# A two-layer block on one core: the delta rule's triangular systems are solved with beta on their diagonal, and the sixteen products with beta, their loads and the scaled copies go

## The chip, the cores and the metric

The kernel runs on one NeuronCore of a Trainium2 chip, in one launch. The metric is device time in microseconds (us); before the change three runs gave 2293.9, 2294.9 and 2297.77, median 2294.9. One more execution was recorded by the hardware profiler, and everything about single instructions comes from that one.

## What is computed

Input x is 1024 tokens by 1024 channels, float32. Two layers follow each other. The first has a mixer (windowed attention with 8 heads beside a gated delta rule with 4 heads of 128 channels, run forward and backward) and a feed-forward of 4096 units; the second has a pooling, a convolution and a stick-breaking attention branch. The change lies in the first layer's mixer, apart from two waits in the second layer. The delta rule, for each direction and head, in chunks:

```
gc    = cumsum(g)                        # log decay, per token
decay = exp(gc[t] - gc[s])   for s <= t
A     = beta[t] * (k k^T)[t,s] * decay   for s < t
T     = (I + A)^-1                       # lower triangular
w     = T (beta * k * exp(gc)),   u = T (beta * v)
v_new = u - w S;   o = (q exp(gc)) S + (q k^T * decay) v_new
S     = S exp(gc[last]) + (k exp(gc[last]-gc))^T v_new
```

The attention's softmax has a sink logit for each head: m = max(row maximum, sink), weights exp(x - m), and exp(sink - m) joins the sum.

## The kernel before, in words

**Engines and order.** Every piece of work is a step with a name and a key, such as `a1` with (direction d, unit i). `second_layer`, `first_layer` and `build` list the steps with an engine, a rank, and where needed a ring of PSUM banks (`ring`, `frees`) and an order on the same engine (`behind`). `Plan.settle` (L258) then plays all steps through with costs out of `Rehearsal` (L130) and a fixed lag per engine (`LAG`, L199): of the steps that can start it takes the earliest, then the lowest rank. What comes out is one fixed order for each of the five engine queues (TensorE, ScalarE `act`, VectorE `dve`, GpSimd `pool`, SyncE `sp`, which issues all DMAs). On the chip each queue runs strictly in that order and waits on semaphores; a step that waits holds up all that stand behind it on its engine. `SHIFT` (L41) adds small numbers to the ranks of certain steps.

**Stages.** P1 are the projections of layer 1, large products in three float32r passes each (L639, L641, L643). They end 306 us into the span. While they run, the decays are computed and the 32 by 32 diagonal blocks of all triangular systems are solved on VectorE (`lmul`, `zi`, `sol`, `zt`), 128 partitions by 32 by 32 for each direction, one column after the other; the inverses go to DRAM and come back (`inv_out`, `inv_in`). From 306 to about 533 us no large product runs: the delta rule's eight units of 128 tokens in two directions and the attention's eight blocks have TensorE for themselves. From 533 us on follow P3 (output projection), the feed-forward, and the second layer, with large products nearly throughout.

**A unit (d, i).** Sixteen of them, two deep in buffers for each direction (`M.unit`, L250):
- loads: `gcl` brings -gc as a row for each head, spread over 128 partitions, into EB; `bel` brings beta in the same way into AT; `kkl` brings k k^T from `kk_scr` into the one tile `kkL`, and waits until the `a1` of the unit before has read that tile (L2386).
- VectorE: `dd` (L1495) forms D from EB and the mask; `a1` (L1500) multiplies AT by kkL; `a2` (L1538) multiplies AT by D; `qkm` (L1545, L1550) does the same for q k^T. ScalarE: `ebx` (L1156, L1158) takes the exponentials of EB and of D, one instruction for each of the four heads.
- `tex` on GpSimd (L2119) spreads the 32-blocks of the inverse into T and its transpose TT. Levels 32 and 64 then join blocks: TensorE `la` (L761 or L768), VectorE `lp`, TensorE `lb`, VectorE `lt` (L1573, L1577), TensorE `lx` (a transpose, L748), ScalarE `ltt` (L1161) back into TT. At the last level `ltt` copies in four instructions, each scaled with one head's beta (L1168); `copy` is L1005 in the profile.
- the chain over units: `cR`, `cr` (L1585), `cT`, `cn`, `crk`, `co`, `cO` (L1596, L1599), `ckd`, `cs` (L1607, L1610). The heads' products all stand under L716, except `co` (L814, L815). The last four units of each direction end with a norm: `gsq` (L1195), `gs` (L825), `gr` (L1009, L1011), `gn` (L1617).

**Attention.** For a block n: `aqk` (L836), `am` (L1629: adds the bias, takes the maximum), `as1` (L1636, L1638, L1639: maximum with the sink, its negative, sink minus maximum), `ae` (L1207), `as2`, `ap` on GpSimd (L2145), `atr` (L844), `atc`, `apv` (L854).

The first steps of `Plan` that matter for both are the lags:

```
LAG = {"pe": 250.0, "act": 200.0, "dve": 150.0, "pool": 150.0, "sp": 1900.0}
```

Of the kernel before, what the change touches and what calls it, by code (L numbers as in the profile page):

```python
# [106 lines left out]
def v4(ps):  # L107
    return ps[:, :].rearrange("p (j c) -> p j c", j=4)
# [238 lines left out]
class Memory:  # L347


    def __init__(self, nc, A, ctx):  # L350
# [9 lines left out]
        def scratch(name, shape):  # L360
            return nc.dram_tensor(name, shape, F32, kind="Internal").ap()
# [34 lines left out]
        self.qk_scr, self.kkL = scratch("qk_scr", [8, 128, 512]), at(220.5, [128, 4, 128])  # L396
# [602 lines left out]
def scalar_engine(e, q, K):  # L999
# [152 lines left out]
    def ebx(d, i):  # L1152
        n = i if d == 0 else 7 - i
        EB, D = M.unit(d, i, "EB"), M.unit(d, i, "D")
        q.wait_ge(done("dd", d, i), done("gd"))
        e.activation(EB[:, :, :], EB[:, :, :], ACT.Exp, scale=-1.0).then_inc(*tick("ebx", d, i))  # L1156
        for j in range(4):
            a = e.activation(D[:, j, :], D[:, j, :], ACT.Exp, bias=G["ngc"][:, n, 4 * d + j:4 * d + j + 1])  # L1158
        a.then_inc(*tick("ebx", d, i))

    def ltt(d, i, l):  # L1161
        n, TT, ps = i if d == 0 else 7 - i, M.unit(d, i, "TT"), K.prep_bank("lx", d, i, l)
        q.wait_ge(done("lx", d, i, l))
# [236 lines left out]
def vector_engine(e, q, K):  # L1400
# [96 lines left out]
    def a1(d, i):  # L1497
        AT = M.unit(d, i, "AT")[:, :, :]
        q.wait_ge(done("kkl", d, i), done("bel", d, i))
        tt(AT, AT, M.kkL[:, :, :], ALU.mult).then_inc(*tick("a1", d, i))  # L1500

    def lmul(d):

        L = M.L[:, d]
        beta = M.gS[:, d, 0, :]
        q.wait_ge(done("lex", d), done("gS", d))
        tt(L, L, beta.unsqueeze(1 if d else 2).broadcast_to([128, 32, 32]), ALU.mult).then_inc(*tick("lmul", d))
        q.wait_ge(part("lmul", (d,), 1), *[done("kk_in", n) for n in range(8)])
        tt(L, L, M.kkS[:, :, :], ALU.mult).then_inc(*tick("lmul", d))

    def zi():

        q.wait_ge(done("cv", 11), *[done("kk_out", n) for n in range(5, 8)])
        e.memset(M.Z[:, :, :, :], 0.0).then_inc(*tick("zi"))
        q.wait_ge(part("zi", (), 1))
        for d in range(2):
            last = e.memset(M.Z[:, d].rearrange("p a b -> p (a b)")[:, 0:1024:33], 1.0)
        last.then_inc(*tick("zi"))
# [448 lines left out]
    def ss(a, i, p_):  # L1967
# [121 lines left out]
    return dict(pads=pads, idle=idle, nacc=nacc, x1l=x1l, cv=cv, kn=kn, ga=ga, gc=gc, gd=gd, lmul=lmul, zi=zi, sol=sol, zt=zt, dd=dd, a1=a1, a2=a2, qkm=qkm, lp=lp, lt=lt, cr=cr, cO=cO, cs=cs,  # L2089
# [114 lines left out]
def sync_engine(e, q, K):  # L2204
# [296 lines left out]
    return dict(wp=wp, wpre=wpre, wpair=wpair, wb=wb, xl=xl, hst=hst, ho=ho, hx2=hx2, c0=c0, c1=c1, x=x, rows=rows, hb=hb, oh=oh, wload=wload, b3=b3, gT_out=gT_out, qa_out=qa_out, z_out=z_out, kk_out=kk_out, kk_in=kk_in, gS=gS, inv_out=inv_out, inv_in=inv_in, gcl=gcl, bel=bel, kkl=kkl, qk_out=qk_out, qk_in=qk_in, abias=abias,  # L2501
# [7 lines left out]
class Kernel:  # L2509
# [347 lines left out]
def signals(B, K):  # L2857
# [19 lines left out]
    g["bel"] = lambda d, i: f"d_be{d}{i % 2}"  # L2877
    g["kkl"] = "d_xl0"
# [16 lines left out]
PARTS = dict(mp=0, fsq=2, wc=2, nr=2, kr=2, gb=5, ebx=2, gr=2, fr=2, qx=2, na=2, nc=2, gq=2, se=2, cv=4, gc=5, gd=2, lmul=2, sol=2, lex=2, zi=2, ge=2, kk_in=4, gS=2, inv_out=4, inv_in=2, as1=2, as2=2, cz=3, pf=2, ss=3)  # L2895
# [3 lines left out]
def first_layer(p, K):  # L2899
# [70 lines left out]
    for i in range(8):  # L2970
        for d in range(2):
# [4 lines left out]
            add("sp", "bel", d, i, rank=r + PREP_RANK.get((d, i), 0))  # L2976
# [158 lines left out]
def second_layer(p, K):  # L3135
# [33 lines left out]
    for i in range(4):  # L3169
# [3 lines left out]
        for p_, (qb, k0, k1) in enumerate(PIECES):  # L3173
# [9 lines left out]
            add("pe", "sv", i, p_, rank=3)  # L3183
# [226 lines left out]
```

## Time and profile before

| | value |
|---|---|
| median of 3 runs | 2294.9 us (2293.9 to 2297.77) |
| profiled execution, first to last instruction (span) | 2291.9 us |
| TensorE matmul busy | 2247.2 us, 98% |
| TensorE weight loads busy | 1785.5 us, 78% |
| VectorE busy | 1594.7 us, 70% |
| ScalarE busy | 1112.9 us, 49% |
| GpSimd busy | 1030.9 us, 45% |
| DMA | 289.43 MB, mean 126 GB/s |

The profile gives no time of its own for the profiled execution beyond its span; the median of the runs is 3.0 us above that. Times in the trace are microseconds from the start of the span. A busy share is that of an engine's instructions, waits of its queue left out. PEclk is the TensorE clock that was granted, as a share of full speed. SPq is the queue that issues DMAs. Square brackets at the end of a row of the timeline give the idle time in front of it and who ended it.

### The profile page before, as it was taken

How to read it: one execution, taken by the hardware profiler on the slowest of the kernel's cores; microseconds unless marked ns; L12 is line 12 of the kernel's file. 1: busy time of each engine (PE TensorE's matmuls, PEld its weight loads, DVE VectorE, ACT ScalarE, POOL GpSimd, SP SyncE). 2: the span in 40 equal slices, each digit the busy share in tenths (PEclk: the TensorE clock that was granted, in tenths of full speed). 3: DMA queues.
4: the chain of work that ended last, by engine and by line, in shares of the span. 5: the costliest groups of instructions: out<-in, count | busy, mean ns of one | idle time of the engine just before them, and what ended most of it. 6: DMA issues, size and time to landing. Idle time of an engine off the chain costs nothing.

```text
span 2291.9 us, 31262 instructions
## 1 busy us (share of the span) xinstructions
PE 2247.2 (98%) x11389; PEld 1785.5 (78%) x11389; DVE 1594.7 (70%) x2217; ACT 1112.9 (49%) x2008; POOL 1030.9 (45%) x643
## 2 busy tenths in 40 slices
PE   9999989999999999999999999999999999999999
PEld 6778867677878888887887777777777888888886
DVE  7865768776596554689449798888888655545745
ACT  5554157674364555444446365645433322225553
POOL 2212245444247666657767211111123765556663
PEclk9999999999999999999999999999999999999999
DMA  4113353344325443955452301111123343338554
GB/s 160 40 44 99 122 177 107 98 139 158 109 93 188 161 152 133 314 173 166 143 170 83 124 29 46 47 46 47 56 79 124 134 143 111 111 133 294 183 171 147
DMA packets 153764, 289.43 MB, mean 126 GB/s; under 512 B 34915, under 2 KB 44387, under 8 KB 153612
## 3 DMA queue, kind: packets, MB, share of 16 engines
q1 hardware_dynamic: 153612, 287.44, 38.3%
q8 instruction: 91, 1.49, 0.3%
q14 instruction: 61, 0.50, 0.1%
HBM read 207.88 MB, written 79.51 MB: 125 GB/s over the span
## 4 chain that ended last, share of the span: by engine, by line
PE 84%; DVE 8%; ACT 2%; issue 2%; DMA 2%; POOL 1%; SPq 0%; DVEq 0%; POOLq 0%; ACTq 0%
PE bank L869 12%; PE bank L871 12%; PE bank L867 12%; PE bank L639 12%; PE bank L643 11%; PE bank L641 11%; PE bank L716 2%; PE bank L932 2%; PE bank L963 1%; PE bank L945 1%; ACT t L1005 1%; DVE t L1434 1%; DVE t L1974 1%; PE bank L836 1%; PE bank L854 1%
## 5 line engine op out<-in xcount | busy, mean ns | idle before, releaser
L2100 POOL TENSOR_TENSOR t<-t,t 128x512 fp32r<-128x512 f32 (+1 forms) x494 | 810.5, 1652 | 1068.3 <-ACT t L1005 1062.1
L1005 ACT ACTIVATE t<-t 128x512 fp32r<-128x512 f32 (+1 forms) x689 | 448.3, 676 | 653.5 <-PE bank L871 276.3
L639 PE MATMUL bank<-t,t 128*128 128x512 f32 x1360 | 548.5, 403 | 0.0
L643 PE MATMUL bank<-t,t 128*128 128x512 f32 x1360 | 531.4, 391 | 1.1 <-DVE t L1434 0.6
L641 PE MATMUL bank<-t,t 128*128 128x512 f32 x1360 | 530.1, 390 | 1.7 <-POOL t L2100 1.7
L867 PE MATMUL bank<-t,t 128*128 128x512 f32 x1316 | 514.2, 391 | 6.2 <-DVE t L1818 4.6
L869 PE MATMUL bank<-t,t 128*128 128x512 f32 x1316 | 513.3, 390 | 1.4 <-POOL t L2100 1.4
L871 PE MATMUL bank<-t,t 128*128 128x512 f32 x1316 | 513.1, 390 | 0.7 <-DVE t L1434 0.7
L639 PEld LDWEIGHTS bank<-t,t 128*128 128x128 f32 x1360 | 255.7, 188 | 62.7 <-issue 12.7
L643 PEld LDWEIGHTS bank<-t,t 128*128 128x128 f32 x1360 | 255.3, 188 | 58.3 <-POOL t L2100 1.3
L641 PEld LDWEIGHTS bank<-t,t 128*128 128x128 f32 x1360 | 255.9, 188 | 56.3 <-issue 4.6
L867 PEld LDWEIGHTS bank<-t,t 128*128 128x128 f32 x1316 | 247.7, 188 | 59.6 <-DVE t L1818 5.0
L869 PEld LDWEIGHTS bank<-t,t 128*128 128x128 f32 x1316 | 247.6, 188 | 54.2 <-POOL t L2100 3.0
L871 PEld LDWEIGHTS bank<-t,t 128*128 128x128 f32 x1316 | 247.6, 188 | 52.4 <-DVE t L1434 1.1
L1434 DVE TENSOR_TENSOR t<-t,t 128x512 fp32r<-128x512 f32 x192 | 193.4, 1025 | 76.0 <-ACT t L1005 75.3
L1005 ACT ACTIVATE t<-bank 128x512 f32<-128x512 f32 (+2 forms) x255 | 143.1, 578 | 200.0 <-PE bank L945 51.4
L2050 DVE TENSOR_TENSOR t<-t,bank 128x512 f32<-128x512 f32 x105 | 70.3, 682 | 108.3 <-PE bank L871 107.9
L1974 DVE TENSOR_TENSOR_SCAN t<-t,t 128x512 f32<-128x512 f32 (+3 forms) x96 | 112.5, 1171 | 3.3
L1425 DVE TENSOR_TENSOR t<-t,t 128x512 f32<-128x512 f32 x55 | 70.2, 1277 | 25.9 <-ACT t L1382 14.8
L1452 DVE SCALAR_TENSOR_TENSOR t<-t,t,t 128x1024 f32<-128x1024 f32 x48 | 76.3, 1593 | 14.1 <-ACT t L1005 12.8
L1734 DVE TENSOR_TENSOR t<-t,bank 128x512 f32<-128x512 f32 x48 | 32.8, 685 | 61.6 <-PE bank L643 54.5
L716 PEld LDWEIGHTS bank<-t,t 128*128 128x128 f32 x416 | 51.8, 197 | 16.8 <-ACT t L1005 4.6
(250 smaller groups left out, 2641.2 us busy)
## 6 DMA issues: line engine op xcount, KB each, us to landing
t<-in_w SPq DMA_DIRECT2D x87, 512.0 KB, 3.6
hid_scr<-t SPq DMA_DIRECT2D x112, 256.0 KB, 2.1
t<-hid_scr SPq DMA_DIRECT2D x112, 256.0 KB, 2.7
t<-in_wf SPq DMA_DIRECT2D x80, 256.0 KB, 3.3
t<-in_wf SPq DMA_DIRECT2D x36, 512.0 KB, 4.5
g_scr<-t SPq DMA_DIRECT2D x36, 512.0 KB, 2.9
t<-g_scr SPq DMA_DIRECT2D x72, 256.0 KB, 3.4
t<-in_wo SPq DMA_DIRECT2D x24, 512.0 KB, 3.6
```

The lines of the kernel that those rows point to most:

```text
L639: e.matmul(ps[:, :], hi[:, w, :], XH[:, x, hs], start=k == 0, stop=False)
L641: e.matmul(ps[:, :], lo[:, w, :], XH[:, x, hs], start=False, stop=False)
L643: last = e.matmul(ps[:, :], hi[:, w, :], XL[:, x, hs], start=False, stop=k == j.nk - 1)
L716: last = e.matmul(ps[:, 128 * j:128 * j + 128], a(j), b(j), start=True, stop=True)
L867: e.matmul(ps, hi, XH, start=start, stop=False)
L869: e.matmul(ps, lo, XH, start=False, stop=False)
L871: return e.matmul(ps, hi, XL, start=False, stop=stop)
L1005: return e.activation(out, in_, ACT.Copy, **kw)
L1434: return tt(out, x, high.bitcast(F32), ALU.subtract)
L1452: stt(y[:, :] if j < 4 else dst, raw[:, j:j + S], w, y[:, :], ALU.mult, ALU.add).then_inc(*tick("cv", m))
L1974: e.tensor_tensor_scan(x[:, ::-1], one_c.broadcast_to([128, nk]), m_[:, ::-1], 0.0, ALU.mult, ALU.add).then_inc(*tick("ss", a, i, p_))
L2100: return e.tensor_tensor(out, x, high.bitcast(F32), ALU.subtract)
```

## The change

- `lmul` multiplies L by beta along its rows for both directions (direction 1 had it along the columns), and `zi` puts beta, out of `gS`, on the diagonal of the start matrix Z instead of 1. The solved blocks are then (I + A)^-1 diag(beta), in a form in which AT needs no beta, and neither does the last copy into TT.
- `bel` and `a1` are gone, sixteen of each. `kkl` loads k k^T straight into AT, with the waits that `bel` had, and in its place in the list; the tile kkL is gone, and `kkl` has semaphores of its own by direction and parity. `a2` waits for `kkl`.
- The last `ltt` is one copy of 128 by 512 instead of four scaled ones of 128 by 128, sixteen times.
- `as1` has two instructions instead of three: the negative sink is made once in `gc` (a sixth instruction there), and min(-max, -sink) gives the negated maximum at once.
- In the second layer `ss` waits for all `st` of the piece two before, not for the last alone, and `sv` is bound to come behind the `sv` of the piece before.
- All ranks and shifts are as they were.

```diff
     def ltt(d, i, l):
-        n, TT, ps = i if d == 0 else 7 - i, M.unit(d, i, "TT"), K.prep_bank("lx", d, i, l)
         q.wait_ge(done("lx", d, i, l))
-        if l < TOP:
-            a = copy(TT[:, :, :], v4(ps))
-        else:
-            for j in range(4):
-                a = copy(TT[:, j, :], ps[:, 128 * j:128 * j + 128], scale=G["beta"][:, n, 4 * d + j:4 * d + j + 1])
-        a.then_inc(*tick("ltt", d, i, l))
+        copy(M.unit(d, i, "TT")[:, :, :], v4(K.prep_bank("lx", d, i, l))).then_inc(*tick("ltt", d, i, l))
...
         e.reciprocal(G["beta"], w[:, :, :]).then_inc(*tick("gc"))
+        ts(M.rows[:, 32:40], M.rows[:, 16:24], -1.0, None, ALU.mult).then_inc(*tick("gc"))
...
-    def a1(d, i):
-        AT = M.unit(d, i, "AT")[:, :, :]
-        q.wait_ge(done("kkl", d, i), done("bel", d, i))
-        tt(AT, AT, M.kkL[:, :, :], ALU.mult).then_inc(*tick("a1", d, i))
...
-        tt(L, L, beta.unsqueeze(1 if d else 2).broadcast_to([128, 32, 32]), ALU.mult).then_inc(*tick("lmul", d))
+        tt(L, L, beta.unsqueeze(2).broadcast_to([128, 32, 32]), ALU.mult).then_inc(*tick("lmul", d))
...
-        q.wait_ge(part("zi", (), 1))
+        q.wait_ge(part("zi", (), 1), done("gS", 0), done("gS", 1))
         for d in range(2):
-            last = e.memset(M.Z[:, d].rearrange("p a b -> p (a b)")[:, 0:1024:33], 1.0)
+            last = e.tensor_copy(M.Z[:, d].rearrange("p a b -> p (a b)")[:, 0:1024:33], M.gS[:, d, 0, :])
...
-        q.wait_ge(done("ebx", d, i), done("a1", d, i))
+        q.wait_ge(done("ebx", d, i), done("kkl", d, i))
         tt(AT, AT, D, ALU.mult).then_inc(*tick("a2", d, i))
...
-        q.wait_ge(done("rows"))
-        tt(sm[:, :, 8:12], sm[:, :, 0:4], sink, ALU.max).then_inc(*tick("as1", n))
+        q.wait_ge(done("rows"), done("gc"))
+        stt(sm[:, :, 12:16], sm[:, :, 0:4], -1.0, below, ALU.mult, ALU.min).then_inc(*tick("as1", n))
         q.wait_ge(part("as1", (n,), 1))
-        ts(sm[:, :, 12:16], sm[:, :, 8:12], -1.0, None, ALU.mult)
-        tt(sm[:, :, 16:20], sink, sm[:, :, 8:12], ALU.subtract).then_inc(*tick("as1", n))
+        tt(sm[:, :, 16:20], sink, sm[:, :, 12:16], ALU.add).then_inc(*tick("as1", n))
...
-            q.wait_ge(done("st", i0, PIECES[p0][0], (PIECES[p0][2] - 1) // 256))
+            q.wait_ge(*[done("st", i0, PIECES[p0][0], g) for g in range(PIECES[p0][1] // 256, (PIECES[p0][2] + 255) // 256)])
...
-    def bel(d, i):
+    def kkl(d, i):
         n = i if d == 0 else 7 - i
-        q.wait_ge(done("gT_out"))
+        q.wait_ge(done("kk_out", n))
         if i >= 2:
             q.wait_ge(done("la", d, i - 2, TOP))
         if i in (1, 2):
             q.wait_ge(*[done(*y) for y in K.p1_x])
         elif i == 0:
             q.wait_ge(*([done("inv_out")] if d else []), done("whi", 21), done("wlo", 21))
-        start(flat(M.unit(d, i, "AT")[:, :, :]), M.row_of(8 * n + 4 * d), "bel", d, i)
-
-    def kkl(d, i):
-        n = i if d == 0 else 7 - i
-        q.wait_ge(done("kk_out", n))
-        if (d, i) != (0, 0):
-            q.wait_ge(done("a1", *((0, i) if d else (1, i - 1))))
-        start(flat(M.kkL[:, :, :]), M.kk_scr[n], "kkl", d, i)
+        start(flat(M.unit(d, i, "AT")[:, :, :]), M.kk_scr[n], "kkl", d, i)
...
-            add("sp", "bel", d, i, rank=r + PREP_RANK.get((d, i), 0))
+            add("sp", "kkl", d, i, rank=r + PREP_RANK.get((d, i), 0))
...
-            add("dve", "a1", d, i, rank=r + PREP_RANK.get((d, i), 0))
-            add("sp", "kkl", d, i, rank=r + PREP_RANK.get((d, i), 0))
...
-            add("pe", "sv", i, p_, rank=3)
+            add("pe", "sv", i, p_, rank=3, behind=[("sv", K.piece_before(12 * i + p_, 1))] if i or p_ else ())
```

## Rows read from the trace of the kernel before

**Rows 1.** The page, busy time of each engine

```profile
PE 2247.2 (98%) x11389; PEld 1785.5 (78%) x11389; DVE 1594.7 (70%) x2217; ACT 1112.9 (49%) x2008; POOL 1030.9 (45%) x643
```

**Rows 2.** Windows by stage: us, busy of each engine (count), PEclk, DMA share, GB/s

```profile
0.00:300.00 300.00, 295.68 (x1398) 234.79 (x1399) 208.38 (x245) 142.80 (x190) 67.43 (x33) 1.00 0.30 96
300.00:545.00 245.00, 223.14 (x1911) 166.84 (x1910) 181.30 (x453) 164.52 (x459) 117.32 (x69) 0.97 0.45 138
545.00:2292.00 1747.00, 1728.34 (x8084) 1383.83 (x8082) 1204.98 (x1520) 805.57 (x1361) 846.13 (x542) 1.00 0.39 130
```

**Rows 3.** TensorE's waits, 300 to 545 us: total, times, longest

```profile
PE bank L768 <- DVE t L1538: 5.2, 1, 5.2
PE bank L716 <- DVE t L1607: 2.9, 1, 2.9
PE bank L836 <- DVE t L1629: 2.5, 3, 1.2
PE bank L825 <- ACT t L1195: 2.5, 1, 2.5
```

**Rows 4.** Timeline, 307 to 320 us, the stretch of the longest wait

```profile
307.32 2.84 SPq L2209 DMA_DIRECT2D t<-gT_scr  x5
312.08 2.76 SPq L2209 DMA_DIRECT2D t<-kk_scr  x1
...
315.45 0.69 DVE L1495 SCALAR_TENSOR_TENSOR t<-t,t 128x512 f32<-128x512 f32 x1 [2.01 <-DMA t<-gT_scr]
316.18 0.63 ACT L1156 ACTIVATE t<-t 128x512 f32<-128x512 f32 x1 [0.90 <-DVE t L1495]
...
318.09 0.60 ACT L1005 ACTIVATE t<-bank 128x512 f32<-128x512 f32 x1
318.83 1.09 PE L768 MATMUL bank<-t,t 64*64 64x64 f32 x8 [5.19 <-DVE t L1538]
319.85 3.76 PE L716 MATMUL bank<-t,t 128*128 128x128 f32 x16
```

**Rows 5.** Timeline, TensorE at full clock

```profile
434.66 2.05 PE L716 MATMUL bank<-t,t 128*128 128x128 f32 x16
```

**Rows 6.** VectorE groups, 255 to 545 us: busy us, mean ns, idle before

```profile
L1500 DVE TENSOR_TENSOR t<-t,t 128x512 f32<-128x512 f32 x16 | 15.6, 975 | 6.4 <-DMA t<-kk_scr 3.3 <-DMA t<-gT_scr 2.9
```

**Rows 7.** VectorE groups, 300 to 545 us

```profile
L1638 DVE TENSOR_SCALAR t<-t 128x8 f32<-128x8 f32 x8 | 3.5, 434 | 0.3
```

**Rows 8.** Timeline, ScalarE: a scaled copy in four instructions

```profile
327.19 1.13 ACT L1005 ACTIVATE t<-bank,t 128x128 f32<-128x128 f32 x4
```

**Rows 9.** Timeline, VectorE and TensorE around the second longest wait

```profile
449.17 1.18 DVE L1638 TENSOR_SCALAR t<-t 128x8 f32<-128x8 f32 x1
...
452.10 1.16 PE L716 MATMUL bank<-t,t 128*128 128x128 f32 x8 [2.90 <-DVE t L1607]
```

**Rows 10.** Timeline, GpSimd and VectorE together

```profile
337.95 3.74 POOL L2145 TENSOR_TENSOR t<-t,t 128x1024 f32<-128x1024 f32 x2 [2.83 <-DVE t L1646]
339.88 2.36 DVE L1500 TENSOR_TENSOR t<-t,t 128x512 f32<-128x512 f32 x1
```

**Rows 11.** Timeline, the two products after kkL loads, direction 1 unit 1

```profile
323.20 0.68 DVE L1500 TENSOR_TENSOR t<-t,t 128x512 f32<-128x512 f32 x1
326.32 0.69 DVE L1538 TENSOR_TENSOR t<-t,t 128x512 f32<-128x512 f32 x1
```

**Rows 12.** Timeline: start matrix Z, load of gS, last copy of unit (0,0)

```profile
198.15 1.76 DVE L1514 MEMSET t<- 128x2048 f32 x1 [5.65 <-DMA kk_scr<-t]
199.08 2.57 SPq L2209 DMA_DIRECT2D t<-gT_scr  x4
...
298.36 1.14 ACT L1005 ACTIVATE t<-bank,t 128x128 f32<-128x128 f32 x4 [3.23 <-PE bank L748]
```

**Rows 13.** Windows of 10 us, same columns as rows 2

```profile
320.00:330.00 10.00, 10.00 (x78) 8.91 (x80) 6.92 (x21) 4.34 (x12) 5.20 (x4) 0.83 0.67 203
450.00:460.00 10.00, 7.90 (x78) 6.36 (x80) 9.04 (x24) 7.67 (x24) 5.43 (x5) 0.83 0.23 78
```

More of the change, by code:

```diff
@@ L395, in __init__ @@
         self.gT_scr, self.bias_scr = scratch("gT_scr", [128, 128]), scratch("bias_scr", [8, 512])
-        self.qk_scr, self.kkL = scratch("qk_scr", [8, 128, 512]), at(220.5, [128, 4, 128])
+        self.qk_scr = scratch("qk_scr", [8, 128, 512])
         self.U = []
@@ L1152, in ebx @@
     def ebx(d, i):
+        EB, D = M.unit(d, i, "EB"), M.unit(d, i, "D")
         n = i if d == 0 else 7 - i
-        EB, D = M.unit(d, i, "EB"), M.unit(d, i, "D")
         q.wait_ge(done("dd", d, i), done("gd"))
@@ L1632, in as1 @@
     def as1(n):
-        sm, sink = M.sm[n % 2], M.rows[:, 16:24].rearrange("p (g j) -> p g j", g=2)
+        sm, (sink, below) = M.sm[n % 2], [M.rows[:, a:a + 8].rearrange("p (g j) -> p g j", g=2) for a in (16, 32)]
         q.wait_ge(*[done("am", g, n, j) for g in range(2) for j in range(4)])
-        q.wait_ge(done("rows"))
-        tt(sm[:, :, 8:12], sm[:, :, 0:4], sink, ALU.max).then_inc(*tick("as1", n))
+        q.wait_ge(done("rows"), done("gc"))
+        stt(sm[:, :, 12:16], sm[:, :, 0:4], -1.0, below, ALU.mult, ALU.min).then_inc(*tick("as1", n))
         q.wait_ge(part("as1", (n,), 1))
-        ts(sm[:, :, 12:16], sm[:, :, 8:12], -1.0, None, ALU.mult)
-        tt(sm[:, :, 16:20], sink, sm[:, :, 8:12], ALU.subtract).then_inc(*tick("as1", n))
+        tt(sm[:, :, 16:20], sink, sm[:, :, 12:16], ALU.add).then_inc(*tick("as1", n))
     def as2(n):
@@ L2087, in ofd @@
         tt(M.xr[:, m, :], M.xr[:, m, :], M.OF[:, m, :], ALU.add).then_inc(*tick("ofd", h, m))
-    return dict(pads=pads, idle=idle, nacc=nacc, x1l=x1l, cv=cv, kn=kn, ga=ga, gc=gc, gd=gd, lmul=lmul, zi=zi, sol=sol, zt=zt, dd=dd, a1=a1, a2=a2, qkm=qkm, lp=lp, lt=lt, cr=cr, cO=cO, cs=cs,
+    return dict(pads=pads, idle=idle, nacc=nacc, x1l=x1l, cv=cv, kn=kn, ga=ga, gc=gc, gd=gd, lmul=lmul, zi=zi, sol=sol, zt=zt, dd=dd, a2=a2, qkm=qkm, lp=lp, lt=lt, cr=cr, cO=cO, cs=cs,
                 gn=gn, am=am, as1=as1, as2=as2, ao=ao, yal=yal, zm=zm, gg=gg, evd=evd, hac=hac, hac2=hac2, x2l=x2l, xn=xn, tx=tx, tl=tl, ws=ws, fu2=fu2, fu3=fu3, fc11=fc11, fu4=fu4, fc22=fc22, fc21=fc21, fc12=fc12, ft3=ft3, ft2=ft2,
@@ L2096, in gpsimd_engine @@
     M, B, p = K.mem, K.bulk, K.plan
-    done, part, tick = p.done, p.part, p.tick
+    C, done, part, tick = M.C, p.done, p.part, p.tick
     def low(out, x, high):
@@ L2113, in tex @@
     def tex(d, i):
-        c, own = M.C32[2 * d + i % 2], M.C("own32").rearrange("p (k b) -> p k b", b=32).unsqueeze(1).broadcast_to([128, 4, 4, 32])
+        c, own = M.C32[2 * d + i % 2], C("own32").rearrange("p (k b) -> p k b", b=32).unsqueeze(1).broadcast_to([128, 4, 4, 32])
         def spread(name, f):
@@ L2499, in o1 @@
         start(K.out[:, m, 512:1024], M.xr[:, m, :], "o1", m)
-    return dict(wp=wp, wpre=wpre, wpair=wpair, wb=wb, xl=xl, hst=hst, ho=ho, hx2=hx2, c0=c0, c1=c1, x=x, rows=rows, hb=hb, oh=oh, wload=wload, b3=b3, gT_out=gT_out, qa_out=qa_out, z_out=z_out, kk_out=kk_out, kk_in=kk_in, gS=gS, inv_out=inv_out, inv_in=inv_in, gcl=gcl, bel=bel, kkl=kkl, qk_out=qk_out, qk_in=qk_in, abias=abias,
+    return dict(wp=wp, wpre=wpre, wpair=wpair, wb=wb, xl=xl, hst=hst, ho=ho, hx2=hx2, c0=c0, c1=c1, x=x, rows=rows, hb=hb, oh=oh, wload=wload, b3=b3, gT_out=gT_out, qa_out=qa_out, z_out=z_out, kk_out=kk_out, kk_in=kk_in, gS=gS, inv_out=inv_out, inv_in=inv_in, gcl=gcl, kkl=kkl, qk_out=qk_out, qk_in=qk_in, abias=abias,
                 aq=aq, aout=aout, ya=ya, zl=zl, hx=hx, xs=xs, plw=plw, ys1=ys1, g_out=g_out, p_out=p_out, s_out=s_out, by=by, bg=bg, gld=gld, xr=xr,
@@ L2876, in signals @@
     g["gcl"] = lambda d, i: f"d_gc{d}{i % 2}"
-    g["bel"] = lambda d, i: f"d_be{d}{i % 2}"
-    g["kkl"] = "d_xl0"
+    g["kkl"] = lambda d, i: f"d_kk{d}{i % 2}"
     g["qk_out"] = lambda d, i: f"d_wb{i}" if d == 0 else f"d_blk{4 + i}"
@@ L2892, in signals @@
     return g
-PARTS = dict(mp=0, fsq=2, wc=2, nr=2, kr=2, gb=5, ebx=2, gr=2, fr=2, qx=2, na=2, nc=2, gq=2, se=2, cv=4, gc=5, gd=2, lmul=2, sol=2, lex=2, zi=2, ge=2, kk_in=4, gS=2, inv_out=4, inv_in=2, as1=2, as2=2, cz=3, pf=2, ss=3)
+PARTS = dict(mp=0, fsq=2, wc=2, nr=2, kr=2, gb=5, ebx=2, gr=2, fr=2, qx=2, na=2, nc=2, gq=2, se=2, cv=4, gc=6, gd=2, lmul=2, sol=2, lex=2, zi=2, ge=2, kk_in=4, gS=2, inv_out=4, inv_in=2, as1=2, as2=2, cz=3, pf=2, ss=3)
 PARTS["or"] = 2
```

2 rows, old and new, of the table SIGNALS are left out of this document.

## The prediction

> **What bounds the kernel.** I read the page first: TensorE's matmuls are busy 2247.2 of 2291.9 us [rows 1]. Nothing in the change takes a matmul away, so all that it can give or take lies in the 44.7 us in which TensorE is not busy, and in the time that it runs at a lower clock. Windows by stage show where these are [rows 2]: 0 to 300 us has 4.3 us of idle TensorE, 300 to 545 us has 21.9, the remaining 1747 us have 18.7. Everything that the change edits in the units and in the attention runs in the middle stage. There the large products are absent, VectorE is busy 181.3 of 245 us and ScalarE 164.5, and only there is the mean granted clock under 1 (0.97).
>
> TensorE's waits in that stage come next [rows 3]. One wait is 5.2 us, one 2.9, one 2.5 (the last norm, L825). The last is L836 behind `am` (L1629), 2.5 us in three waits. The ten smaller groups of the view have 8.4 us, which makes 21.5, the idle time of the stage but for 0.4. In those ten VectorE has 0.7 us, ScalarE 5.2 in eight waits of at most 1.0, the rest are loads and TensorE itself. So without the 5.2 and the last norm's 2.5, waits behind VectorE are 6.1 us (2.9 + 2.5 + 0.7), behind ScalarE 5.2.
>
> The 5.2 us wait is named after `a2` (L1538), but the timeline shows a second thing that ended with it [rows 4]: a ScalarE copy out of a bank, 318.09 to 318.69, 0.14 us ahead of the matmul. By the order in the code that is `qkc`, which frees the bank that `lb` needs. It stands behind `ebx` on ScalarE, that waits for `dd` (L1495), and `dd` for a load of gT_scr that came at 315.4 us; it is one of the burst of five issued between 307.3 and 310.2, behind the last large product. Behind the wait sixteen L716 matmuls took 3.76 us, where sixteen at full clock took 2.05 [rows 4, 5]; the window 320 to 330 stands at 0.83 [rows 13].
>
> **Part by part.**
>
> `a1` goes: sixteen instructions, 15.6 us of VectorE busy [rows 6], fourteen of them in the stage. The third instruction of `as1` goes: eight of L1638, 3.5 us [rows 7]. Of the two that stay one changes from two operands to three at 128 by 8; I take no difference (bounds: 0.1 us either way for each, eight times, from the two small forms around it). `gc` gets one more instruction of 8 columns at 189 us, where VectorE waits for others: nothing; if uncovered, 0.2 us once. VectorE so loses about 19 us of work, a tenth of what it does in the stage.
>
> How much of the 15.6 is work? An `a1` took 0.68 us alone [rows 11] and 2.36 beside a GpSimd product of 3.74 us [rows 10]. Sixteen at 0.68 are 10.9, so 4.7 us are time in which the instruction stood. That time may pass to the instruction that comes next: I count 11 to 15.6 us and use it only as a share, so the sum hardly moves. The Trainium skill, in SBUF — State Buffer, "SBUF: two separate sides", says that the port pair which VectorE and GpSimd share is an exclusive lock, held for a whole instruction, and that a VectorE instruction with two SBUF inputs blocks against a GpSimd one that reads SBUF. By that rule the 4.7 us are not saved where `a2` or `qkm`, with two SBUF inputs too, takes the place of `a1` beside the same GpSimd product; VectorE's gain would be 11 us and not 15.6.
>
> `ltt` at the last level: four scaled copies take 1.13 us together, one whole copy 0.60 [rows 4, 8]. Sixteen times 0.53 is 8.5 us of ScalarE, a twentieth of its work in the stage, and 0.53 us on the way from `lx` to `cT` of each unit.
>
> Loads: sixteen `bel` of 256 KB go, with their issues on SyncE. `kkl` is now where `bel` was and waits for no `a1`. At the burst this changes little in front: still one `gcl` and one 256 KB load into AT for each unit ahead of the `gcl` on which `dd` waits. So I leave the 5.2 us wait and its slow clock where they are, value 0; bounds 0 and -6.9 (5.2 + 3.76 - 2.05). What does move is unit (1,1): its k k^T load is issued at 312.08, after the bias loads, since kkL was not free [rows 4]; its `a1` ran at 323.2 and its `a2` at 326.3 [rows 11]. In the place of `bel` it is issued near 308 and should be there with the others near 315 to 316, so `a2` of that unit can come some 8 us earlier. TensorE is busy 10.0 of 10 us from 320 to 330 [rows 13], so this is spare time first, and pays only where TensorE waits later.
>
> `zi` now waits for gS, which is issued from 199.1 to 201.7 [rows 12]. The plan will put the step later, and its memset of 1.76 us may then lie ahead of the first `lmul` instead of in an idle stretch. The solve ends at most 1.8 us later. What hides that: unit (0,0) had its last copy done at 299.5 [rows 12], and its chain starts only behind the last large product near 306. So it costs 0, and at most 1.8 if that cover were gone. `lmul` has the same shape: nothing. The waits added in `ss` are on steps that TensorE does in this order anyway, and `sv` was already in the order of pieces: nothing, bound 0.5 us each way.
>
> **The sum.** The 2.9 us wait ended with `cs` (L1607), and L1638, 1.18 us long, stands in VectorE's unbroken run ahead of it [rows 9]: 1.2 us less. The window there is at clock 0.83 [rows 13]; with a shorter wait between none and the 1.7 us (3.76 - 2.05) that the clock cost behind the longest wait comes back: I take 0.4, near the lower end, since the wait gets shorter and does not go. The remaining 3.2 us behind VectorE and 5.2 behind ScalarE (8.4) shrink with the load. Bounds: 0 if each is set by TensorE's own result, 8.4 if all go. A tenth and a twentieth less work let me take a sixth: 1.4. Together 1.2 + 0.4 + 1.4 = 3.0 us. The span goes from 2291.9 to 2288.9; the median of the runs lies 3.0 us above the span, so 2291.9 us.
>
> **Rivals.**
> (B) *The freed load pays in full.* The plan is made anew, `a2` of (1,1) and all that hangs on it come 8 us earlier, `qkc` slips in front of `ebx`. For it: ScalarE stood idle from 315.28 to 316.18 for that `dd` [rows 4]; if the bank was full by then, a copy put there ends at 315.9 and not at 318.7, 2.8 us earlier. Of the 8.4 us of waits below, 4 could go instead of 1.4, which is 2.6 more. Against: ranks are the same, and `ebx` had the better claim before. 3.0 + 2.8 + 2.6 is 8.4 us: 2286.5.
> (C) *A new in-order wait.* One queue gets a step whose load lands later than the plan holds. The plan counts 1.9 us and the bytes from issue to landing, the load behind the longest wait took between 5 and 8 (issued in the burst from 307.3 to 310.2, there at 315.4). Without `a1`, nothing separates the arrival of k k^T from `a2`, and VectorE's queue is re-sorted, so `a2` or a `dd` can come to stand ahead of an `am`, a `cr` or a `cs` on which a bank depends. It decides where the load lands over 2 us after its place in the queue is reached. One such wait is priced by the one in the trace: 5.2 us and 1.7 of slow clock, 6.9 us. Time 2301.8. For it: the stage has three such waits already, so the order is near this edge. Against: VectorE and the DMA queues have less to do.
> (D) *Nothing.* TensorE is 91% busy in the stage, and most waits follow TensorE's own results within a unit; the units run two deep, so the freed time is slack. 2294.9, within 1.5 us.
> (E) By the lock rule alone VectorE gains 11 us instead of 15.6. The sixth above would be a seventh, 0.2 us: no case of its own.
>
> **How the numbers follow.** A change within 0.2% (4.6 us) can't be told from none. Forecast 0.40 (2288 to 2296; of it 0.14 below 2290.3, 0.26 within), B 0.22 (all faster), C 0.26 (0.25 slower, 0.01 within), D 0.12 (all within). Faster 0.36, same 0.39, slower 0.25. The range from 2284 (B with another 2 us out of the 8.4) to 2302 leaves about 0.06 below and 0.13 above, where C with more than one wait lies. The likeliest case alone spans 2288 to 2296.
>
> **What would show it.** VectorE's busy time near 1576 to 1580 us, ScalarE's near 1104, TensorE's within 3 us of 2247. Right: idle TensorE from 300 to 545 near 19 us, the wait of 5 us behind the third `dd` still there, L1607's wait near 1.7. B: that wait near 2, the stage's idle time under 14. C: a wait of TensorE above 3 us at a new place, with a window at 0.83 behind it. `zi` wrong: the first `inv_out` more than 2 us later and a wait right after 306. The forecast fails altogether if the stages after 545 us differ by more than 3 us, since I hold them to be untouched.

## The result, and the profile after

The change makes the kernel slower: 2310.6 us (median of 4 runs, 2309.2 to 2312.0) against 2294.4 us beside it (4 runs), a ratio of 1.0065 with a 95% interval of 1.0053 to 1.0077. The forecast was 2291.9 us, its range ended at 2302, and it had the change faster, not slower.

The page of the kernel after, busy times (columns as in [rows 1]):

```profile
span 2309.2 us, 31162 instructions
PE 2250.1 (97%) x11389; PEld 1788.1 (77%) x11389; DVE 1587.6 (69%) x2194; ACT 1104.9 (48%) x1960; POOL 1035.7 (45%) x643
```

The work did get less: VectorE 7.1 us below [rows 1], ScalarE 8.0. Of the 17.3 us by which the span grew, 14.4 are idle TensorE (59.1 against 44.7) and 2.9 are TensorE's matmuls at a lower clock. Windows of the kernel after, the last as long as that of [rows 2]:

```profile
0.00:300.00 300.00, 292.95 (x1365) 231.68 (x1365) 208.08 (x240) 140.92 (x185) 69.30 (x33) 0.99 0.28 94
300.00:562.30 262.30, 228.76 (x1935) 171.95 (x1936) 173.98 (x438) 158.99 (x417) 119.13 (x70) 0.95 0.37 116
562.30:2309.20 1746.90, 1728.38 (x8091) 1384.52 (x8089) 1205.59 (x1518) 804.95 (x1359) 847.26 (x540) 1.00 0.38 130
```

The last row has TensorE as busy as that of before, to 0.1 us: nothing is lost behind the middle stage. In the first row TensorE is idle 7.1 us, not 4.3; in the second 33.5, not 21.9. TensorE's waits in the kernel after, 310 to 560 us (columns: what, the releaser, us in total, times, longest):

```profile
PE bank L716 <- ACT t L1005: 7.2, 1, 7.2
PE bank L768 <- ACT t L1005: 4.9, 1, 4.9
PE bank L825 <- ACT t L1189: 4.1, 2, 2.7
PE bank L844 <- ACT t L1005: 3.6, 3, 1.3
PE bank L836 <- DVE t L1619: 3.3, 4, 1.2
PE bank L768 <- DVE t L1549: 2.6, 2, 2.4
```

Set beside [rows 3], the long wait at the burst is still there (4.9), the 2.9 behind `cs` is not in the list, and a wait of 7.2 us is new. I use two marks that every trace has: the end of P1's last large product and the first large product of P3 (L639). They stand at 305.96 and 532.84 before, at 310.46 and 552.20 after. So P1 ends 4.5 us late, the stage takes 241.7 and not 226.9 us (14.9 more), and the rest is 2.1 us shorter.

**Where P1 loses.** Timeline of the kernel after, VectorE and below it TensorE (start, length, engine, line; in brackets the idle time ahead and its releaser):

```profile
281.30 0.48 DVE L1489 MEMSET t<- 128x512 f32 x1 [8.90 <-DMA inv_scr<-t]
281.71 0.63 DVE L1490 SCALAR_TENSOR_TENSOR t<-t,t 128x512 f32<-128x512 f32 x1
282.25 0.68 DVE L1692 SCALAR_TENSOR_TENSOR t<-bank,t 128x512 f32<-128x512 f32 x1
288.04 0.48 DVE L1489 MEMSET t<- 128x512 f32 x1 [5.11 <-DMA t<-gT_scr]
288.44 0.63 DVE L1490 SCALAR_TENSOR_TENSOR t<-t,t 128x512 f32<-128x512 f32 x1
288.98 0.68 DVE L1692 SCALAR_TENSOR_TENSOR t<-bank,t 128x512 f32<-128x512 f32 x1
289.58 0.68 DVE L1528 TENSOR_TENSOR t<-t,t 128x512 f32<-128x512 f32 x1
...
292.79 1.12 PE L761 MATMUL bank<-t,t 64*64 64x64 f32 x16 [2.75 <-POOL t L2108]
```

`dd(1,0)` (288.04) stands ahead of an eviction of P1 (L1692) and of `a2(0,0)` (L1528). Its load is not there, and VectorE stands for 5.1 us with both behind it. Before, the same stretch reads:

```profile
283.54 1.37 DVE L1538 TENSOR_TENSOR t<-t,t 128x512 f32<-128x512 f32 x1 [0.91 <-ACT t L1158]
284.84 0.68 DVE L1550 TENSOR_TENSOR t<-t,t 128x512 f32<-128x512 f32 x1
287.12 0.48 DVE L1494 MEMSET t<- 128x512 f32 x1 [1.60 <-DMA t<-gT_scr]
```

There `a2(0,0)` ran 6 us earlier, in the time in which `dd(1,0)` had to wait anyway. TensorE's wait at 292.79 is named after GpSimd's `tex`; experiment 2 shows that it goes when this one step is moved back. It is rival C, a `dd` ahead of what others need, at a place that I had not looked at.

**Where the stage's end loses.** The chain of waits of the kernel after (start, length, what):

```profile
533.42 0.52 ACT t L1189
...
536.01 0.64 ACT t L1011
...
536.68 1.72 DVE t L1607
...
538.49 2.65 DVE t L1657
...
541.16 1.12 ACT t L1005 x2
...
542.33 2.09 PE bank L716 x8
```

and the timeline of the same stretch, ScalarE and TensorE:

```profile
536.55 2.08 ACT L1005 ACTIVATE t<-t 128x1024 fp32r<-128x1024 f32 x3
541.16 0.63 ACT L1005 ACTIVATE t<-t 128x512 fp32r<-128x512 f32 x1 [2.54 <-DVE t L1657]
541.70 0.58 ACT L1005 ACTIVATE t<-bank 128x512 f32<-128x512 f32 x1
542.33 2.08 PE L716 MATMUL bank<-t,t 128*128 128x128 f32 x8 [7.21 <-ACT t L1005]
```

TensorE's `cT(1,7)` (L716 at 542.33) needs `ltt(1,7)`, a copy of 0.58 us out of a bank (541.70). ScalarE's queue has that copy behind casts for P3, behind the norm of another unit, and directly behind the cast `zh(1,0)` (541.16), which itself waits for VectorE's `zm` (L1657). A copy on the last unit's chain waits for work that P3 needs later. Before, `ltt(1,7)` stood right behind `gr(0,7)`. The window from 540 to 550 us has clock 0.58:

```profile
540.00:550.00 10.00, 5.63 (x24) 5.17 (x24) 8.52 (x7) 5.36 (x9) 8.71 (x6) 0.58 0.51 183
```

All five queues came out in another order in the stage, though no step had another rank. `settle` takes the step that can start first, so every duration and every wait that the change edits can move the order of other steps. For example `tex(0,2)` now comes ahead of `tex(0,1)`, and `la` of unit (0,2) ahead of that of (0,1).

### The profile page after: what moved, and what is told of

Read it like the earlier page. It is cut to its first block, busy times and chain, and to the rows that moved or that the text cites. A ratio compares the mean times of both kernels' runs of the same rounds, so it can differ in the third digit from the quotient of the medians.

```text
span 2309.2 us, 31162 instructions
## 1 busy us (share of the span) xinstructions
PE 2250.1 (97%) x11389; PEld 1788.1 (77%) x11389; DVE 1587.6 (69%) x2194; ACT 1104.9 (48%) x1960; POOL 1035.7 (45%) x643
## 4 chain that ended last, share of the span: by engine, by line
PE 84%; DVE 8%; ACT 3%; issue 2%; DMA 2%; POOL 1%; SPq 0%; DVEq 0%; ACTq 0%; POOLq 0%
PE bank L867 12%; PE bank L869 12%; PE bank L871 12%; PE bank L639 12%; PE bank L643 11%; PE bank L641 11%; PE bank L716 2%; PE bank L932 1%; PE bank L963 1%; PE bank L945 1%; ACT t L1005 1%; DVE t L1428 1%; DVE t L1963 1%; PE bank L836 1%; ACT t L1201 1%
## 5 line engine op out<-in xcount | busy, mean ns | idle before, releaser
L639 PE MATMUL bank<-t,t 128*128 128x512 f32 x1360 | 548.8, 404 | 0.5 <-ACT t L1005 0.5
L643 PE MATMUL bank<-t,t 128*128 128x512 f32 x1360 | 531.7, 391 | 0.6 <-POOL t L2089 0.5
L639 PEld LDWEIGHTS bank<-t,t 128*128 128x128 f32 x1360 | 256.0, 188 | 63.9 <-issue 13.6
L643 PEld LDWEIGHTS bank<-t,t 128*128 128x128 f32 x1360 | 255.7, 188 | 57.7 <-POOL t L2089 1.4
L641 PEld LDWEIGHTS bank<-t,t 128*128 128x128 f32 x1360 | 256.3, 188 | 55.9 <-issue 4.6
L867 PEld LDWEIGHTS bank<-t,t 128*128 128x128 f32 x1316 | 247.4, 188 | 59.3 <-DVE t L1807 5.0
L871 PEld LDWEIGHTS bank<-t,t 128*128 128x128 f32 x1316 | 247.3, 188 | 53.3 <-DVE t L1428 1.4
L869 PEld LDWEIGHTS bank<-t,t 128*128 128x128 f32 x1316 | 247.4, 188 | 52.4 <-POOL t L2089 1.6
L1005 ACT ACTIVATE t<-bank 128x512 f32<-128x512 f32 (+3 forms) x271 | 152.6, 580 | 216.8 <-PE bank L945 51.4
L1446 DVE SCALAR_TENSOR_TENSOR t<-t,t,t 128x1024 f32<-128x1024 f32 x48 | 76.3, 1593 | 14.2 <-ACT t L1005 12.9
L716 PE MATMUL bank<-t,t 128*128 128x128 f32 x416 | 59.7, 292 | 9.5 <-ACT t L1005 7.2
```

Source lines behind the costliest of these rows:

```text
L639: e.matmul(ps[:, :], hi[:, w, :], XH[:, x, hs], start=k == 0, stop=False)
L641: e.matmul(ps[:, :], lo[:, w, :], XH[:, x, hs], start=False, stop=False)
L643: last = e.matmul(ps[:, :], hi[:, w, :], XL[:, x, hs], start=False, stop=k == j.nk - 1)
L716: last = e.matmul(ps[:, 128 * j:128 * j + 128], a(j), b(j), start=True, stop=True)
L867: e.matmul(ps, hi, XH, start=start, stop=False)
L869: e.matmul(ps, lo, XH, start=False, stop=False)
```

## Experiments

In nine of these kernels the order and the PSUM banks come from a list and no longer from `settle`; ltt_plan, a_thr and retuned have their order from `settle`. The code cut (the end of `settle`):

```
+        order = self.take_written()     # a list for each of the five queues
         self.order = order
```

Each ratio is against the kernel before, run beside it; its median was 2295.0 us beside the experiments 1 to 4, 2296.5 beside 5 to 8 and 2295.9 beside 9 to 12. So kernels of different groups are compared by their ratios.

**1. old_order.** The changed kernel in the order of before: `kkl` in the place of `bel`, `a1` taken out, nothing else moved but `zi`, which goes behind the eviction next to it, since it now needs a load.

> The changed kernel, but every engine queue in the order that the kernel before had (a1 left out, the load of k k^T where bel stood, evd27 ahead of zi); the PSUM bank of each step as before. Nothing else differs from the changed kernel. Theory (the work was saved, the 16 us are the new order alone): 2288 to 2294 us, so at or just under the kernel before. Rival (the changed work itself costs: the load straight into AT, zi behind gS, or the new waits): 2300 us or more, and the stage from 306 us on as long as in the changed kernel.

Measured: 2291.7 us (11 runs), ratio 0.9987, interval 0.9978 to 0.9995. The same instructions are 18 us faster than in their own order. The whole loss is in the new order and the banks that go with it. Against the kernel before 3.0 us are won, by the interval 1 to 5. The stage takes 224.2 us, and TensorE is idle in 18.9 us of it (before: 21.3).

**2. dd10_back.** After's own order; one step moved.

```
 dve: ... evd(41) [dd(1,0) out of here] evd(42) a2(0,0) qkm(0,0)
+     dd(1,0)
```

> The changed kernel in its own order, with one VectorE step moved: dd(1,0) goes from ahead of evd42 and a2(0,0) to behind qkm(0,0), where it stood before. Theory (VectorE stood 5.1 us for the load of dd(1,0) with a2(0,0) behind it, so TensorE waited 2.75 us and then ran slowly): the wait before the first L761 goes, the last large product of P1 ends near 306 instead of 310.5, time 4 to 5 us shorter, 2306. Rival (that wait is cover for something else, or comes back at the next load): under 1.5 us.

Measured: 2308.1 us (2306.6 to 2309.1), ratio 1.0055, interval 1.0041 to 1.0069. The span of the profiled execution is 4.6 us shorter than that of after, the wait of 2.75 us fell to 0.64, and P1 ended at 307.05. The medians give 2.5 us, and the two intervals overlap, so they do not show the gain by themselves. The place is right; the price, between the theory and its rival, is settled by start_new below.

**3. ltt_back** and **4. both_back.** One step moved on ScalarE, without and with the move of 2.

```
+act: gsq(0,7) ltt(1,7) yah(1,3) ... gr(0,7) ... zh(1,0)
-act: gsq(0,7) yah(1,3) ... gr(0,7) ... zh(1,0) ltt(1,7)
```

> The changed kernel in its own order, with one ScalarE step moved: ltt(1,7,1) goes from behind zh(1,0) to right behind gsq(0,7). Theory (TensorE's 7.2 us wait at 535 us is this copy, queued behind six steps of the next stage, of which zh(1,0) itself waits for VectorE): that wait goes, time 5 to 8 us shorter, 2303 to 2306. Rival (the end of the stage is set by the y pieces, that is by zm, zh and the GpSimd differences, so that the wait only moves to the first P3 products): 0 to 2 us.

> Both moved steps together. Theory: the two add, 9 to 13 us shorter, 2298 to 2302. Rival: one of them hides the other, no more than the larger of the two alone.

Measured: 2312.5 us (ratio 1.0074, 1.0059 to 1.009) and 2309.6 us (1.0061, 1.0047 to 1.0075), neither told apart from after. My theories fell: no gain shows, which is what the rivals had for the time, though the wait moved to another step than the first rival named. The timeline of ltt_back, TensorE:

```profile
543.11 0.77 PE L991 MATMUL bank<-t,t 128*128 128x128 f32 x2 [8.61 <-ACT t L1182]
550.39 2.08 PE L1002 MATMUL bank<-t,t 128*128 128x512 f32 x2 [3.52 <-ACT t L1366]
```

The 7.2 us wait is gone, and one of 8.6 us stands at `co(1,7)` (L991, which is L814 with the lines shifted), since `cn(1,7)` is behind the same casts. The whole chain of the last unit is late in that queue, not one step of it.

**5. tail_old, 6. tail_new, 7. start_new.** All three have the instructions of after. Each has the order of one kernel up to one point of time, and behind it the relative order of the other; the points are the end of P1 and a place shortly before the end of the stage.

```
tail_old:   after's order   | cut near the stage's end | before's
tail_new:   before's order  | cut near the stage's end | after's
start_new:  after's order   | cut at the end of P1     | before's
```

> The changed kernel, all its instructions, and its own order of the queues until shortly before the end of the middle stage; the steps behind that point (the last units' chain, the last two norms, the yah and zh casts, the first steps of P3) come in the relative order that they had in the kernel before. THEORY: the tail order is most of the loss; in it ScalarE had ltt(1,7), cn(1,7) and the last norm behind casts for later products, and TensorE stood 7.2, 0.8 and 2.7 us where the kernel before had one 2.5 us wait. So 8 to 11 us go: 2299 to 2302. RIVAL 1: the tail is late because the units before it are late (the unit order was changed, 11.8 and 9.4 us of idle TensorE there), and the tail's wait only shows it: gain under 3 us, 2307 to 2311. RIVAL 2: as ltt_back and both_back showed for single steps, the wait moves on to the next step: gain 3 to 6 us.

> The mirror image of tail_old: the changed kernel with the order of before until shortly before the end of the middle stage, and from there on the relative order of the changed kernel. THEORY: the tail costs 8 to 11 us also where everything ahead of it is in the old order: 2300 to 2303, against 2291.7 for old_order. RIVAL 1 (the tail only shows an earlier delay): within 2 us of old_order, 2290 to 2294.

> The changed kernel with its own order until the last large product of P1 (all that stands there in the queues, dd(1,0) ahead of the last evictions included), then the order of before. THEORY: the part in P1 costs what dd10_back gave back and the traces show, 2.5 to 4.6 us: 2294 to 2297 against 2291.7 for old_order. RIVAL: it is hidden, since the middle stage has slack that takes up a late start: 2291 to 2293.

Measured: tail_old 2303.7 us, ratio 1.0034 (1.0022 to 1.0045); tail_new 2308.6, 1.0052 (1.0037 to 1.0067); start_new 2297.8, 1.0005 (0.9996 to 1.0015). The first came out 2 us above its theory, the second 6 us above, and start_new 1 us above. TensorE in tail_new:

```profile
536.76 2.08 PE L893 MATMUL bank<-t,t 128*128 128x128 f32 x8 [7.21 <-ACT t L1182]
539.62 0.77 PE L991 MATMUL bank<-t,t 128*128 128x128 f32 x2 [0.78 <-ACT t L1182]
545.87 2.08 PE L1002 MATMUL bank<-t,t 128*128 128x512 f32 x2 [2.49 <-ACT t L1366]
```

With everything ahead of it in the order of before, the tail has the same waits as in the kernel after: it makes its own loss. Steps of the ratio share the 18 us (0.0078) out, in units of 0.001: old_order to start_new 1.8 (4 us, P1), start_new to tail_old 2.9 (7 us, the middle), tail_old to after 3.1 (7 us, the tail). These are single differences with intervals of about 3 to 4 us each way.

The parts do not add. Put onto the old order, the tail costs 15 us, and the two marks, each from one profiled execution, show why it is more than its share:

| kernel | P1 ends | P3 starts | stage, us | idle TensorE in it |
|---|---|---|---|---|
| before | 305.96 | 532.84 | 226.9 | 21.3 |
| old_order | 307.05 | 531.24 | 224.2 | 18.9 |
| start_new | 310.93 | 534.89 | 224.0 | 19.1 |
| tail_old | 308.19 | 539.21 | 231.0 | 25.7 |
| tail_new | 305.67 | 546.95 | 241.3 | 32.7 |
| after | 310.46 | 552.20 | 241.7 | 33.4 |

With the new tail the stage is as long as in after, whether the middle has the old order (tail_new) or the new one (after). The middle's 7 us show only where the tail is the old one. So the 18 us are P1 and the tail, 4 and 15 us with their intervals, and what the middle costs disappears behind the tail. In tail_old the idle time added in the middle, against old_order, lies between 400 and 520 us (10.8 against 4.5), not before 400 us (11.9 against 11.5), where units (0,1) and (0,2) changed places.

**8. ltt_plan and 9. ltt_old.** The kernel before with the single copy for the last `ltt`; beta is left out of the second factor. ltt_plan has the order made anew, ltt_old that of before.

```
-            for j in range(4):
-                a = copy(TT[:, j, :], ps[...], scale=G["beta"][...])
+        copy(M.unit(d, i, "TT")[:, :, :], v4(K.prep_bank("lx", d, i, l)))
```

> The kernel before with one edit alone: the last copy into TT is one instruction of 128 by 512 and not four scaled ones (beta is left out of the second factor, so part of the computation is missing), and the order of all queues is made anew from the same ranks with that shorter step. Strictly less work than before: ScalarE loses 8.5 us. THEORY: the loss comes from the new order and not from what the change adds, so a small edit with a new order can be slower than before as well: 2297 to 2306, with a wait of over 3 us at a new place in the middle stage. RIVAL: it takes a0 large edit like the whole change to upset the order; less work makes it no slower: 2291 to 2295.

> The same instructions as ltt_plan (the kernel before with the last copy into TT as one instruction of 128 by 512; beta is left out of the second factor), but every queue in the order that the kernel before has. THEORY: the 24 us that ltt_plan lost are the order alone. With the old order the shorter copy gives 0 to 3 us: 2291 to 2296, and the waits of TensorE in the middle stage are those of the kernel before within 0.5 us each. RIVAL: the shorter copy itself disturbs something (a bank freed at another time, VectorE and ScalarE at one bank): 2300 or more.

Measured: ltt_plan 2319.4 us, ratio 1.010 (1.0085 to 1.0115); ltt_old 2295.0, 0.9998 (0.9989 to 1.0007). One step was made 0.53 us shorter, sixteen times, ScalarE has 7 us less work, and the kernel is 23 us slower than before; the same instructions in the old order are as fast as before. So it does not take a large edit to lose by the new order. The windows of ltt_plan between its marks (stage, rest):

```profile
305.54:550.19 244.65, 214.60 (x1836) 160.09 (x1837) 169.03 (x438) 148.87 (x398) 104.71 (x62) 0.95 0.41 127
550.19:2316.20 1766.01, 1742.90 (x8128) 1393.71 (x8126) 1223.52 (x1534) 814.91 (x1376) 857.73 (x549) 0.99 0.39 130
```

The stage takes 17.8 us more than before, and 30.1 us of it are idle. P1 ends as early as before, and here the order disturbs the start of P3 as well: the rest is 7 us longer. I had expected 2297 to 2306 us and one new wait over 3 us. The time is 13 us above that, and there is no such wait; new are 2.5 us (L748), 2.5 (L643) and 2.2 (L768) and many of about 1. Its wait of 2.7 us at L716 (452.13 us) is the one behind `cs` that before has at 452.10, 2.9 us long [rows 9].

**10. a_thr.** After, with one wait more on the load, order made anew.

```
 def kkl(d, i):
+        if (d, i) != (0, 0):
+            q.wait_ge(done("a2", *((0, i) if d else (1, i - 1))))
```

> The changed kernel with one wait more: the load of k k^T of a unit waits until a2 of the unit before it (in the order (0,0), (1,0), (0,1), ...) has run, as it had waited for a1 in the kernel before; and the order of the queues is made anew. THEORY 1: that wait had kept the units in their sequence, and its loss is what turned the order of the middle stage (tex(0,2) ahead of tex(0,1), la of (0,2) ahead of (0,1)); with it back 5 to 9 us return: 2301 to 2306, where tail_old left 7 us between 320 and 520. THEORY 2: any new order differs in many places, so it is as likely to lose elsewhere: 2304 to 2315, with a wait over 3 us at yet another place.

Measured: 2307.2 us, ratio 1.0055 (1.0042 to 1.0069), not told apart from after. The units are in their old sequence again (`tex(0,1)` ahead of `tex(0,2)`), and the time is not back: beside the wait at the burst (4.1 us) there are new ones of 3.1 and 3.0 us, both at L716. In P1 VectorE stands for the load of `dd(1,0)` again, 4.6 us, and P1 ends at 309.87. Theory 2 holds. With the wait back on `kkl` the units keep their sequence, so its loss is what had turned it; that this sequence costs the 7 us of the middle is not shown.

**11. h_qkc.** old_order with one move.

```
+act: qkc(0,2) ebx(0,2)
-act: ebx(0,2) qkc(0,2)
```

> The changed kernel in the order of before, with a single move: on ScalarE the copy of q k^T of unit (0,2) out of its bank goes ahead of the two exponentials of unit (0,2), that wait for the third load of gT_scr in the burst behind P1. THEORY (rival B of the prediction): the copy ends 2.8 us earlier, the wait of 5.3 us near 318 shrinks to 2.5, and part of the slow clock behind it goes: 2 to 4 us below old_order, 2288 to 2290. RIVAL: a2 is a second reason for the same wait, 0.1 us earlier; then nothing changes: 2291 to 2292.5.

Measured: 2292.1 us (11 runs), ratio 0.9988 (0.9979 to 0.9997), the same as old_order. ScalarE of h_qkc first, of old_order below:

```profile
316.67 0.60 ACT L1182 ACTIVATE t<-bank 128x512 f32<-128x512 f32 x1 [1.51 <-DMA z_scr<-t]
317.17 0.62 ACT L1333 ACTIVATE t<-t 128x512 f32<-128x512 f32 x1
```
```profile
317.09 0.63 ACT L1333 ACTIVATE t<-t 128x512 f32<-128x512 f32 x1 [0.75 <-DVE t L1667]
317.63 1.26 ACT L1335 ACTIVATE t<-t,t 128x128 f32<-128x128 f32 x4
318.79 0.57 ACT L1182 ACTIVATE t<-bank 128x512 f32<-128x512 f32 x1
```

The copy ended 2.1 us earlier, after a wait of 1.5 us of its own, and the matmul's wait went from 5.35 to 4.02. P1 had ended 1.2 us earlier in this execution, so about 0.9 us of the 2.1 belong to the move. The stage took 224.0 us against 224.2: what was won there was lost again further on. The first term of rival B, 2.8 us, gives nothing here.

**12. retuned.** The changed kernel, its order made by `settle`, with other numbers in `SHIFT` for the steps of the stage (641 entries in all, 55 before, found by a search in which the kernel's own plan was to end the stage early; the entries of other steps stayed, but for `abias`). The first of them:

```
-SHIFT = {("abias",): 1.5, ("apv", 1): 1.25, ("atr", 3): -1.5, ...
+SHIFT = {('a2', 0): 10.25, ('a2', 0, 0): 1, ('a2', 0, 2): -0.25, ('a2', 0, 3): -1, ...
```

> The changed kernel as it is, with other values in SHIFT for the steps of the middle stage: values for which the kernel's own plan puts the end of that stage earliest. Only ranks differ, no instruction. THEORY: the loss comes from ranks that were fitted to the durations of the kernel before; fitted to those of the changed kernel they give at least what old_order gave, and more: 2278 to 2290, with idle TensorE from 300 to the end of the stage under 15 us. RIVAL: the plan's cost of a load (1.9 us, where 5 to 8 were seen in the burst) is wrong just where it matters, so a tighter plan breaks on the chip: 2295 to 2310.

Measured: 2289.9 us (11 runs, 2288.0 to 2292.4), ratio 0.9976 (0.9967 to 0.9985): the fastest kernel of this study, faster than before, not told apart from old_order. Idle TensorE from 300 to 545 us is 19.2 us, not under 15, and the wait at the burst is 4.4 us. The time lies at the very top of its range (2278 to 2290).

## Why the prediction was wrong, step by step

**The step that failed** is that the sum has no term for the new order of the queues. The forecast took the waits of before, shortened each a little, and left the new order to rival C, at a chance of 0.26 and one wait's price, 6.9 us. The runs show that term to be 18 us (0.0078, after against old_order), against 3.0 us saved by the work. The ground given for leaving it out did not hold: "ranks are the same", said of B, and for C "VectorE and the DMA queues have less to do". Nothing in the trace of before made an order as good as the old one likely: three of the four new orders that `settle` made here lost 16 to 23 us against the same work in the old order (after 18, a_thr 16, ltt_plan 23). Only the one whose shifts were fitted to the new durations did not. By these four, C should have had the largest chance.

**The price of C.** 6.9 us for one wait was low. The kernel has C in two places that the runs separate, P1 (4 us) and the tail (7 us taken out of after, 15 us put onto the old order); 7 us of the middle show only without the new tail. "A wait above 3 us at a new place" came true at the tail (7.2).

**The sum.** 3.0 us in all was met by old_order (ratio 0.9987 is 3.0 us), but by luck, since its terms were not met.
- The 1.2 us of L1638 failed. The timeline of old_order, VectorE, GpSimd and TensorE at the place of [rows 9]:

```profile
445.19 4.16 POOL L2285 TENSOR_TENSOR t<-t,t 128x512 f32<-128x512 f32 x3 [0.63 <-DVE t L1712]
...
446.94 1.23 DVE L1803 SCALAR_TENSOR_TENSOR t<-t,t 128x8 f32<-128x8 f32 x1
448.20 1.17 DVE L1805 TENSOR_TENSOR t<-t,t 128x8 f32<-128x8 f32 x1
449.30 0.67 DVE L1766 TENSOR_TENSOR t<-t,bank 128x512 f32<-128x512 f32 x1
...
451.06 1.86 PE L893 MATMUL bank<-t,t 128*128 128x128 f32 x8 [2.83 <-DVE t L1774]
```

and in the kernel before:

```profile
446.15 4.16 POOL L2119 TENSOR_TENSOR t<-t,t 128x512 f32<-128x512 f32 x3 [0.63 <-DVE t L1545]
...
450.26 0.15 DVE L1639 TENSOR_TENSOR t<-t,t 128x8 f32<-128x8 f32 x1
```

The last instruction of `as1` (L1805) took 0.15 us before and takes 1.17 now, in the place of the one that was removed. It ends at 449.37, just where the run of three GpSimd products ends (445.19 + 4.16 = 449.35). The wait stayed: 2.83 against 2.90. So 128 by 8 numbers took 1.2 us because the instruction stood until that product ended, and the standing passed on. By the Trainium skill's SBUF — State Buffer, "SBUF: two separate sides", a VectorE instruction with two SBUF inputs, as L1805 is, and a GpSimd one that reads SBUF exclude each other for whole instructions on the port pair that they share. These rows agree. I had used that rule for `a1` only, and not for my own 1.2 us.
- The 0.4 us of clock behind that wait were not won either: the window from 450 to 460 us stands at 0.83 in old_order too.
- Smaller waits: forecast 1.4. By pieces of the stage, idle TensorE fell from 12.9 to 11.5 us up to 400 us and from 5.7 to 4.5 from there to 520, so 2.6. The share of a sixth was low. My reading of these waits was also off: in the ten small groups VectorE has 1.3 us, not 0.7 (0.6 us in front of L643 were left out), and ScalarE's 5.2 us are nine waits, not eight. A sixth of 9.0 would be 1.5.

**VectorE's load.** Forecast 1576 to 1580 us, measured 1582.5 in old_order and 1587.6 after. The three small instructions of `as1` together took 9.0 us and the two take 7.4 in old_order: 1.6 saved, not 3.5. (In the order of after they take 4.5.) With these 1.6 and the 10.9 us that sixteen `a1` would take alone, I estimate 12.5 us saved, and old_order has 12.2 us less than before: the 4.7 us in which `a1` stood were not saved. After has 2.6 us more in `zi` than old_order. VectorE and GpSimd, after and then old_order:

```profile
203.65 3.77 POOL L2100 TENSOR_TENSOR t<-t 128x1024 f32<-128x1024 f32 x2
...
204.04 3.44 DVE L1507 COPY t<-t 128x32 f32<-128x32 f32 x2 [1.12 <-DMA t<-gT_scr]
```
```profile
203.86 3.80 POOL L2277 TENSOR_TENSOR t<-t 128x1024 f32<-128x1024 f32 x2 [0.35 <-DMA t<-gT_scr]
...
205.13 0.78 DVE L1684 COPY t<-t 128x32 f32<-128x32 f32 x2 [2.39 <-DMA t<-gT_scr]
```

Both kernels have the copies beside the two GpSimd products, but at another moment. After: they start 0.4 us behind the first product and end with the second (207.48 against 207.42). In old_order they start 1.3 us behind it; the first copy takes 0.69 us and ends with the first product (205.82 against 205.77), and the second takes 0.18.

**Right.** ScalarE near 1104 (1104.9). The wait at the burst stays (4.9 after, 5.35 in old_order). `zi` costs nothing that shows: in old_order P1 ends at 307.05, in h_qkc, with the same order there, at 305.87, before at 305.96, so this mark moves by 1.2 us with one order (by 2.7 us, 308.19 to 310.93, between kernels that have the P1 of after). The stages behind were within 3 us in after, as held (2.1 shorter).

**Rival B** is refused by h_qkc in its first term, and no run had its 8.4 us; retuned came to about 5.5 us below before (ratio 0.9976).

## What to carry to other kernels

Where a program orders its queues from durations, an edit has two effects, the work and the new order, and they have to be weighed and measured apart: pin the old order first, then let it be made anew with the shifts fitted again. A new order lost 16 to 23 us here in three cases out of four, against a few us of work saved. Four cases in one kernel are few; they show that the risk is larger than the gain, not how large it is elsewhere. Moving one late step of the tail forward only moved the wait to the next step of the same late chain. Before an instruction is counted as a gain, see whether it worked or stood: if it ends with another engine's instruction, the next one will stand in its place.

## What had not been expected of the hardware

Two copies of 128 by 32 numbers (L1507) took 1.56 and 1.97 us in after, each until one of GpSimd's products ended; in old_order, which reached them 1.1 us later, the second took 0.18 us.

Waits can cost twice, but by no fixed rate. ltt_plan has 8.8 us more idle TensorE in the stage than before and 9.0 us more of matmul busy time there, at a mean clock of 0.95 against 0.97, for the same matmuls (1836 records in both). After has 12.1 us more idle time in the stage and only 2.8 us more busy time, at 0.96. What decides between the two is not shown.
